# Attention in a streaming encoder layer: every third key tile of the longer groups copied out raw by ScalarE and split by GpSimd

## The reference, cut to what matters

```python
rel = relu(einsum('bthd,bsd->bths', iq, ik));  score = einsum('bths,bth->bts', rel, iw)
_, sel = lax.top_k(where(visible, score, -inf), topk)        # at most 256 keys for each query
logits = einsum('btgrd,btkgd->btgrk', qg, k[sel]) * HEAD_DIM ** -0.5 - slope * abs(q_pos - sel)
out = einsum('btgrk,btkgd->btgrd', softmax(where(valid, logits, -inf)), v[sel])
...
merged = ga * ((o_a * silu(za)) @ w_a) + gb * ((o_b * silu(zb)) @ w_b) + gc * ((o_c * silu(zc)) @ w_c)
x = x + merged @ w_out
```

## Time and profile before

| | |
|---|---|
| median of the runs | 2805.56 us |
| profiled execution: time, span | 2803.79 us, 2802.0 us |
| PE, PEld busy | 2679.1 us (96%), 2475.7 us (88%) |
| DVE, ACT, GpSimd busy | 2056.7 us (73%), 1417.9 us (51%), 1250.9 us (45%) |
| low halves (L2305): count, busy | 290, 192.8 us |
| high halves (L2241): count, busy | 290, 167.1 us |
| score units on DVE (L2283): count, busy | 344, 217.3 us and 27.9 us for reading the minimum |

### The profile page before, as it was taken

How to read it: one execution, slowest core, us unless ns; L and a number is a source line. 1 busy time by engine, 2 the same in 40 slices (tenths; PEclk the granted TensorE clock), 3 DMA queues, 4 the chain that set the end, 5 groups by cost and what they waited for, 6 DMA issues and landing times. The chain is left out here.

```text
span 2802.0 us, 40012 instructions
## 1 busy us (share of the span) xinstructions
PE 2679.1 (96%) x14029; PEld 2475.7 (88%) x14029; DVE 2056.7 (73%) x4123; ACT 1417.9 (51%) x2425; POOL 1250.9 (45%) x846
## 2 busy tenths in 40 slices
PE   6999999999999999999998788999989998999998
PEld 6999999999999999999998666777879997888886
DVE  6477899999999999852735578899976557555554
ACT  5377578776777778853222566777740002111111
POOL 1100288686878778783455363322253332111110
PEclk9999999999999999999999899999999999999999
DMA  4433323233433232234655532212165555122211
GB/s 170 123 117 123 126 97 119 94 123 108 131 105 122 71 138 96 91 121 136 196 158 165 152 97 73 71 50 59 49 241 160 182 172 180 49 73 74 66 57 38
DMA packets 271430, 320.35 MB, mean 114 GB/s; under 512 B 36609, under 2 KB 234753, under 8 KB 270589
## 3 DMA queue, kind: packets, MB, share of 16 engines
q1 hardware_dynamic: 170691, 189.97, 22.2%
q10 hardware_dynamic: 100538, 127.82, 13.0%
HBM read 196.36 MB, written 120.73 MB: 113 GB/s over the span
## 5 line engine op out<-in xcount | busy, mean ns | idle before, releaser
L1659 PE MATMUL psum<-hT_hi,j_whi 128*128 128x416 f32 x2440 | 870.1, 357 | 2.7 <-issue 2.6
L1659 PE MATMUL psum<-hT_hi,j_wlo 128*128 128x416 f32 x2440 | 857.4, 351 | 0.0
L1659 PE MATMUL psum<-hT_lo,j_whi 128*128 128x416 f32 x2440 | 856.4, 351 | 0.0
L1273 POOL TENSOR_TENSOR v_y<-v_y,v_product 128x422 f32<-128x422 f32 x459 | 554.1, 1247 | 87.4 <-ACT v_product L1255 87.4
L448 DVE TENSOR_SCALAR_CACHE_REDUCE s_tie<-s_key,s_bits 128x640 bf16<-128x640 f32 (+14 forms) x352 | 464.3, 1319 | 12.3
L1659 PEld LDWEIGHTS psum<-hT_hi,j_whi 128*128 128x128 f32 x2440 | 459.3, 188 | 12.2 <-issue 4.7
L1659 PEld LDWEIGHTS psum<-hT_lo,j_whi 128*128 128x128 f32 x2440 | 460.6, 189 | 9.2 <-issue 1.6
L1659 PEld LDWEIGHTS psum<-hT_hi,j_wlo 128*128 128x128 f32 x2440 | 459.2, 188 | 5.7
L1255 ACT ACTIVATE v_product<-v_x,v_taps 128x422 f32<-128x422 f32 x510 | 302.7, 641 | 86.0 <-POOL v_y L1273 57.2
L1521 ACT ACTIVATE j_out<-psum 128x416 f32<-128x416 f32 x285 | 144.5, 508 | 339.0 <-PE psum L1659 327.1
L1468 POOL TENSOR_TENSOR j_wlo<-j_w,j_whi 128x1024 fp32r<-128x1024 f32 x61 | 151.5, 2484 | 341.3 <-ACT j_whi L1503 341.2
(11 more groups left out here) (294 smaller groups left out, 4892.4 us busy)
## 6 DMA issues: line engine op xcount, KB each, us to landing
T_dram<-j_out ACTq DMA_DIRECT2D x59, 624.0 KB, 2.9
j_w<-in_w_in ACTq DMA_DIRECT2D x59, 512.0 KB, 3.8
m_gate<-T_dram SPq DMA_DIRECT2D x60, 416.0 KB, 3.5
T_dram<-j_out ACTq DMA_DIRECT2D x59, 416.0 KB, 2.4
m_oraw<-B_dram SPq DMA_DIRECT2D x15, 832.0 KB, 5.4
M_dram<-m_merged ACTq DMA_DIRECT2D x5, 1664.0 KB, 7.4
n_x<-in_x_prompt SPq DMA_DIRECT2D x16, 512.0 KB, 5.4
f_mraw<-M_dram SPq DMA_DIRECT2D x16, 512.0 KB, 4.8
```

What stands on the lines that cost most here:

```text
L1273: pool.tensor_tensor(y[k % 2][:], y[k % 2][:], product[n % RING][:], ALU.add).then_inc(added, 1)
L1659: last = pe.matmul(bank, w[p][:, k, :], h[:, k, t0:t0 + SPAN], start=(k == 0 and q == 0), stop=(k == KD - 1 and q == 2))
```

## The change

In groups with more than seven key tiles, except the two of t = 14, the tiles kt = 5, 8, 11 and 14 (as far as there are such) go another way. ACT copies the PSUM bank out raw, as float32, into one buffer; GpSimd makes both halves from it, the high half by adding zero, the low half by a subtraction; DVE skips them. The raw buffer is the last 128 columns of four heads of `L`, which queries up to t = 13 don't use, and for i = 15 and 16 the last 512 columns of `nd[0]`. As there is one buffer, ACT waits with a raw copy until GpSimd is through with the one before (`raw_read`). On GpSimd the first such tile of a group stands ahead of `gate` and `end`, the others behind them.

```diff
-    L = [scores(f"a_l{h}", [P, SEQ]) for h in range(HEADS)]
+    every_l = scores("a_l", [P, HEADS, SEQ])
+    L = [every_l[:, h, :] for h in range(HEADS)]
...
+    NO_ROOM = (TILES - 3,)
...
-        group.tiles = []
-        for kt in range(-(-group.keys // P)):
+        group.tiles, group.by_pool = [], []
+        count = -(-group.keys // P)
+        for kt in range(count):
             u = ring % RING
+            if count > HALF - 1 and group.i not in NO_ROOM and kt >= 5 and kt % 3 == 2:
+                group.by_pool.append(kt)
+                group.tiles.append((kt, min(P, group.keys - kt * P), u, in_slot[u], weighed_in_slot[u], ring, raws))
+                raws += 1
+            else:
...
+    def raw_of(group):
+
+        return every_l[:, 0:4, SEQ - P:SEQ] if group.i < TILES - 3 else nd[0][:, SEQ - 512:SEQ].rearrange("q (h n) -> q h n", h=4)
...
+        def low(group, x):
+            kt, w, u, nu, nk, n, raw = group.tiles[x]
+            values = raw_of(group)[0:w]
+            hi, lo = (buf[u][0:w, :].rearrange("q (h n) -> q h n", h=4) for buf in (pT_hi, pT_lo))
+            pool.wait_ge(raw_made, raw + 1)
+            if nk:
+                pool.wait_ge(pv_used[u], nk)
+            pool.tensor_tensor(hi, values, c.zero[0:w].unsqueeze(2).to_broadcast([w, 4, P]), ALU.add).then_inc(raw_hi, 1)
+            pool.wait_ge(raw_hi, raw + 1)
+            pool.tensor_tensor(lo, values, f32(hi), ALU.subtract).then_inc(pt_free[u], 1)
+            pool.wait_ge(pt_free[u], nu + 1)
+            pool.sem_inc(raw_read, 1)
+
         for group in groups:
             if group.n in LATE_GROUPS:
                 late_split(group.n - LATE_GROUPS[0])
             if group.g == 1 and 0 < group.i < TILES - 2:
                 split(group.i + 2)
+            for x in group.by_pool[:1]:
+                low(group, x)
             if group.n:
                 gate(groups[group.n - 1])
                 end(groups[group.n - 1])
+            for x in group.by_pool[1:]:
+                low(group, x)
             if group is last_prompt:
                 pool.wait_ge(qk_full, last_prompt.units[-1][6] + 1)
                 split_input(c, pool, 0)
...
         def turned(group, x):      # ScalarE
...
             act.wait_ge(pt_full, n + 1)
+            if x in group.by_pool:
...
+                if number:
+                    act.wait_ge(raw_read, number)
+                act.activation(raw_of(group)[0:w], c.psum[0:w, PT[u], :].rearrange("q (h n) -> q h n", h=4), ACT.Copy).then_inc(raw_made, 1)
+                return
...
             for ahead in range(3) if x == 0 else (x + 2,):      # VectorE
-                if ahead < len(group.tiles):
+                if ahead < len(group.tiles) and ahead not in group.by_pool:
                     low(group, ahead)
```

More of the change, by code:

```diff
@@ L1876, in stage_attend @@
     rs_cleared, rs_made = S("a_rs_cleared"), S("a_rs_made")
+    raw_made, raw_hi, raw_read = S("a_raw_made"), S("a_raw_hi"), S("a_raw_read")
     exp_done, rs_ready, pt_full, pt_hi, o_copied, factor_made = (
@@ L1896, in stage_attend @@
     CACHE_GROUPS = range(20, 24)
-    units = ring = keys = 0
+    units = ring = keys = raws = 0
+    NO_ROOM = (TILES - 3,)
     in_slot, weighed_in_slot = [0] * RING, [0] * RING
@@ L1905, in stage_attend @@
                 units += 1
-        group.tiles = []
-        for kt in range(-(-group.keys // P)):
+        group.tiles, group.by_pool = [], []
+        count = -(-group.keys // P)
+        for kt in range(count):
             u = ring % RING
-            group.tiles.append((kt, min(P, group.keys - kt * P), u, in_slot[u], weighed_in_slot[u], ring, keys))
-            in_slot[u], weighed_in_slot[u], ring, keys = in_slot[u] + 1, weighed_in_slot[u] + 1, ring + 1, keys + 1
+            if count > HALF - 1 and group.i not in NO_ROOM and kt >= 5 and kt % 3 == 2:
[3 more added lines that the diff above has]
+            else:
+                group.tiles.append((kt, min(P, group.keys - kt * P), u, in_slot[u], weighed_in_slot[u], ring, keys))
+                keys += 1
+            in_slot[u], weighed_in_slot[u], ring = in_slot[u] + 1, weighed_in_slot[u] + 1, ring + 1
         group.cached = None
@@ L2236, in turned @@
         def turned(group, x):
-            kt, w, u, nu, nk, n, _ = group.tiles[x]
+            kt, w, u, nu, nk, n, number = group.tiles[x]
             act.wait_ge(pt_full, n + 1)
+            if x in group.by_pool:
+                if number == 0:
+                    act.wait_ge(late_ready, len(late_splits))
+                    act.wait_ge(operands, len(splits))
+                if number:
+                    act.wait_ge(raw_read, number)
+                act.activation(raw_of(group)[0:w], c.psum[0:w, PT[u], :].rearrange("q (h n) -> q h n", h=4), ACT.Copy).then_inc(raw_made, 1)
+                return
             if nk:
```

## The result

| | before | after |
|---|---|---|
| median of 6 runs each, us | 2805.61 (2803.87 to 2806.16) | 2819.73 (2818.86 to 2826.94) |
| profiled execution, us (span) | 2803.79 (2802.0) | 2820.11 (2818.3) |
| low halves on VectorE | 290 | 246 |

The ratio is 1.0055, with an interval of 1.0042 to 1.0068: the change costs 14.1 us. The forecast was +6.2, with a range up to 2820. The sign was right, and the loss is more than twice the forecast's. The time lies 0.3 us inside the range.

A forecast was written before the change was run, and what follows sets the result against it. The prediction took TensorE and VectorE as nearly full together in groups 14 to 27, VectorE ending last. A 17.2 us later stage end less 11 net gain gave +6.2 us: median 2811.8 us, range 2802 to 2820.

The forecast's parts named there:

- What bounds the kernel: Groups 14 to 27: TensorE and VectorE nearly full together, VectorE ending last; weight loads wait 35.2 us for it.
- The gain of 12 us in groups 14 to 27: 32 low halves fewer on VectorE, 19.2 us of its pace; 12 us gained, ends 4 and 19.2.
- ACT's copy at nothing: ScalarE's raw copy: same input, size and engine, so no cost; its wait for the raw buffer over in time except at the end.
- GpSimd's pair at 2.45 us: Each moved tile on GpSimd: zero add 1.04, subtraction 1.28, two hand-overs of 0.07; 2.8 us as the other end.
- Losses at tile 8: Groups 30 and 31: tile 8 late because its copy stands behind a long exponential; 0.9 and 1.6 us lost.
- The end of the stage: From tile 14 of group 31, GpSimd's queue of moved tiles and merge operands makes the last weighing 17.2 us later.
- some 9 us in each: Groups 32 and 33: TensorE was to wait for GpSimd some 9 us in each.
- At a fixed distance: After the last weighing: output product, store, splitting and next TensorE work follow unchanged, so the 17.2 us delay carries through whole.
- The sum: Whole kernel: 17.2 us lost at the end less 11 net gained before, +6.2 us; predicted median 2811.8.
- (B): Rival: GpSimd late in every group, 0.5 us at 20 tiles, taking 10 of the gain; 2822 us, chance 0.16.
- (A): Rival: VectorE's relief in groups 14 to 27 and 30 fully shortens the stage; -4.4 us, 2801, chance 0.18.
- (C): Rival: the shift at the stage's end is taken up and costs nothing, the gain stands; 2795 us, chance 0.06.

The follow-up runs named there:

- the first experiment: The change applied in groups 14 to 27 alone (32 tiles), the last four groups as in the kernel before: 2805.16 us against 2804.95, ratio 0.9998.

## Why the prediction was right in sign and wrong in size

**What bounds the kernel: right as a statement, read too coarsely.** VectorE does end last for TensorE in groups 14 to 27, but only at some steps of a group, and which ones was not read. The prediction's own numbers had a sign of it: for group 26 it had 20.4 us of VectorE and 19.1 of TensorE, and the group took 21.40. Neither sum fills the group; each engine waits for the other in turn.

**The gain of 12 us in groups 14 to 27: the step that failed.** It was worked out by group sums: VectorE's 20.4 us against TensorE's pace of 19.1, so up to 1.3 gained in group 26. Measured there is 0.2 (21.20 us in the first experiment's trace for 21.40). The gain with nothing in the tiles' place is 2.4 us in all 14 groups, and with GpSimd in their place nothing. (TensorE's pace was put too low as well: group 30, which it bounds, takes 22.11 us for 16 tiles, 1.38 a step and not 1.31.) The start of group 25 shows why. First the kernel before:

```profile
1891.40 0.61 DVE L2283 CUSTOM_DVE_ANT_0 a_l<-psum,a_nd 128x448 f32<-128x448 f32 x1
1892.08 0.47 PE L2188 MATMUL psum<-a_khi,a_qs 128*128 128x448 f32 x1 [0.62 <-DVE a_lows L2283]
...
1892.85 0.68 DVE L2305 TENSOR_TENSOR a_ptlo<-psum,a_pthi 128x512 fp32r<-128x512 f32 x1
...
1895.25 0.67 DVE L2283 CUSTOM_DVE_ANT_0 a_l<-psum,a_nd,a_lows 128x448 f32<-128x448 f32 x1
...
1895.85 0.68 DVE L2305 TENSOR_TENSOR a_ptlo<-psum,a_pthi 128x512 fp32r<-128x512 f32 x1
...
1895.98 0.47 PE L2188 MATMUL psum<-a_khi,a_qs 128*128 128x448 f32 x1 [0.54 <-DVE a_lows L2283]
```

TensorE waits twice, 0.62 and 0.54. The second wait is for the score unit of 1895.25, behind which the low half of tile 5 stands (1895.85), the first that the change takes away. It comes after both waits on VectorE's queue and can't shorten either. A third wait, at the last score units of the group, does have the low halves of tiles 5, 8 and 11 ahead of it, but it is short: 0.28 us before and 0.22 after (first and second row):

```profile
1906.63 0.47 PE L2188 MATMUL psum<-a_khi,a_qs 128*128 128x448 f32 x1 [0.28 <-DVE a_lows L2283]
```

```profile
1907.59 0.47 PE L2219 MATMUL psum<-a_khi,a_qs 128*128 128x448 f32 x1 [0.22 <-DVE a_lows L2322]
```

Tile 3's low half (1892.85) stands ahead of the second wait. The same place after the change:

```profile
1893.22 0.47 PE L2219 MATMUL psum<-a_khi,a_qs 128*128 128x448 f32 x1 [0.60 <-DVE a_lows L2322]
...
1896.40 0.67 DVE L2322 CUSTOM_DVE_ANT_0 a_l<-psum,a_nd,a_lows 128x448 f32<-128x448 f32 x1
...
1897.00 0.61 DVE L2322 CUSTOM_DVE_ANT_0 a_l<-psum,a_nd 128x448 f32<-128x448 f32 x1
1897.12 0.47 PE L2219 MATMUL psum<-a_khi,a_qs 128*128 128x448 f32 x1 [0.53 <-DVE a_lows L2322]
...
1897.97 0.68 DVE L2322 CUSTOM_DVE_ANT_0 a_l<-psum,a_nd,a_lows 128x448 f32<-128x448 f32 x1 [0.36 <-PE psum L2220]
```

The waits are the same (0.60 and 0.53); the unit of 1897.00 now follows at once, and VectorE spends what it saved on waiting for TensorE (0.36). It can't save the time up for a later wait, as there are only two PSUM banks for score units. And with tile 3 moved:

```profile
1882.74 1.04 POOL L2120 TENSOR_TENSOR a_pthi<-a_l,zero 128x512 fp32r<-128x512 f32 x1 [0.60 <-ACT a_l L2276]
...
1883.44 0.47 PE L2219 MATMUL psum<-a_khi,a_qs 128*128 128x448 f32 x1 [0.60 <-DVE a_lows L2322]
...
1886.74 0.19 PEld L2219 LDWEIGHTS psum<-a_khi,a_qs 128*128 128x128 f32 x1 [0.40 <-DVE a_lows L2322]
1886.74 0.48 PE L2219 MATMUL psum<-a_khi,a_qs 128*128 128x448 f32 x1
```

The first wait stays. At the second the matmul waits no more (the last row has no bracket), though its weight load still waits 0.40 beside the matmul ahead; from the first waiting product to this one it takes 3.30 us instead of 3.90 (1886.74 - 1883.44; 1895.98 - 1892.08). Fourteen times 0.6 is 8.4; the groups gained 9.8, nine of them 0.5 to 0.6 each, four 0.8 to 1.4, and group 22, where no matmul had waited for a score unit, nothing. The prediction had said that "the DVE work at the group's start stays and the relief comes from step 3 on", and priced that as "some of that not". It was nearly all of it. The low end it gave for this term, 4, was too high as well, and one of its own signs of being wrong, groups 14 to 27 shortened by less than 5, is what came.

**ACT's copy at nothing**: right within groups 14 to 27, where no wait for the raw buffer shows. In groups 31, 32 and 33 ScalarE waited 2.71, 5.54 and 3.42 us for it.

**GpSimd's pair at 2.45 us**: by form, the zero adds and the subtractions are

```profile
L2122 POOL TENSOR_TENSOR a_ptlo<-a_l,a_pthi 128x512 fp32r<-128x512 f32 x32 | 41.4, 1292 | 2.5
...
L2120 POOL TENSOR_TENSOR a_pthi<-a_l,zero 128x512 fp32r<-128x512 f32 x32 | 33.3, 1040 | 101.7 <-ACT a_l L2276 100.9
```

so 1.04 and 1.29, a hand-over of 0.07 or 0.08 between them, and 0.24 before the next item: 2.64 from the start of one item to that of the next (2041.00 - 2038.36). That is 0.2 over the 2.45. VectorE's low halves take 0.68. The Trainium skill ("GPSIMD Engine Reference", section 4.1) puts GpSimd at about half of VectorE's speed with two inputs; the subtraction here takes 1.9 times as long as VectorE's (which has one operand in PSUM), and this agrees. Its other half, one input at about line rate, would have made the chain at the end shorter by under 2.5 us; the chain came out as long as the zero-add row said, and that figure bears only on operations that truly have one input.

**Losses at tile 8**: 1.6 forecast in group 31; tile 8 was weighed at 2034.07 for 2030.45, and 1.7 of these 3.6 us come from the group's later start, so 1.9 measured. In group 30 0.9 forecast, 0.8 measured. Right.

**The end of the stage: right, to 0.9 us.** From the start of group 31 (which is 1.7 us later than before) the last weighing came 18.1 us later; the forecast was 17.2. The chain from the input's split to the last weighing was to take 39.8 us, and took 40.1 (2041.00 to 2081.15), as GpSimd went from item to item without a gap of more than 0.24. The four waits sum to 12.7 us, where "some 9 us in each" of the two groups was said: with no gain before, TensorE came to these tiles later, and so waited less for the same end.

**"At a fixed distance": wrong by 2.8 us.** Store to next work took 22.2 us before (2086.96 - 2064.79), and 19.4 after. Its landing took 5.0 us before and 2.2 after: the eight loads of weight rows, issued 5 to 9 us ahead of it, ran beside it before (261 GB/s while it landed) and had ended after (30 GB/s). The two halves of the end bear this out: with only groups 30 and 31 changed the loads are issued 6 to 10 us ahead of the store and it landed in 4.5 us; with only groups 32 and 33 changed, 15 to 19 us ahead, and it took 2.2.

**The sum.** In the profiled executions: 17.2 for the end was 18.1; the gain of 12, less 0.9, was a loss of 1.7, of which 1.6 is the clock's in group 20; from the last weighing to the store it took 0.5 more, as the last weighing ran at the lower clock; the landing gave 2.8 back, and the rest of the program 1.3 more, which no run here explains. That is +16.3, as the spans have it, and +14.1 in the medians. The 1.3 is less than what executions differ by there: from the last store to the end it took 737.2 us in the kernel before, 737.5 with groups 14 to 27 alone and 740.2 with tile 3, all with the same code from there on. With nothing for the term that failed, the prediction's own sum gives 17.2 + 0.9 = 18.1, and less the 2.8 of the landing 15.3, where the change in groups 30 to 33 alone measured 15.8.

Of the rivals, (B), GpSimd late in every group, has about the right time (2822) by the wrong way: TensorE's weight loads wait 1.6 us for GpSimd there, not 10. (A) falls with the 2.4 us. (C), that the shift at the end is taken up, holds for 2.8 of 17.2.

The Trainium skill ("Perfetto Trace Analysis", section "Identifying the Most-Contended Engine") says to optimize the engine with the highest occupancy first, and in "Optimization Strategy" to look for the gaps on the engine that one optimizes for and what ends them. Applied to VectorE alone, the first would speak for any low half alike. The runs bear out the second, taken for TensorE's gaps: with VectorE busier by 7 us, the kernel that removes what stands ahead of a gap is the faster one.

## What to carry to other kernels

Taking work from an engine is worth what it takes out ahead of a point where another engine waits for it, not its share of a period's sum. List for one period when the bound engine waits, and which items stand on the other's queue between its last idle moment and that wait; only these are candidates. Before work goes to an engine that has idle time on average, read what its in-order queue holds at the end of the stage, since there each item can cost its full length.

## What the runs showed of the hardware

- GpSimd's split of a tile of 32 partitions took as long as one of 128 (1.03 us for the zero add at 2078.74, 1.04 at 2073.43): here 96 partitions less saved 0.01 us.
- GpSimd waits for the end of both instructions of a pair. The subtraction came 0.07 to 0.08 us after the zero add; the next item came 0.24 us after the subtraction, behind which GpSimd also raises a semaphore.
- The same store of 64 KB landed in 5.0 us beside eight loads of weight rows and in 2.2 us alone.
- After waits of 4.92 and 1.79 us TensorE had stretches at 1.2 GHz: the granted clock of 2061.01 to 2081.90 is 0.75 of its 2.4 GHz, and the last weighing took 0.79 us where it had taken 0.49. It cost little here, as TensorE waited for GpSimd anyway: 0.5 us, from the last weighing to ScalarE's copy of the output, 1.25 us (2081.15 to 2082.40) where it had been 0.76.
- Group times repeat closely from execution to execution: group 31 took 21.11 us before, and 21.06 to 21.11 in every kernel that changes nothing in it. A difference of a few tenths of a microsecond in a group can be read from one trace each, where times of the whole program differ by some microseconds.
